# Moving four half turns of expert work out of the query stage, and the prompt's pick into a block of its own

## What is computed

```python
p = rmsnorm(x, ln1) @ w_in                       # qA kA vA | qB kB vB | f | gA gB
yA = band_attention(...); yB = fox_attention(...)
m = sigmoid(gA) * (yA @ w_br_a) + sigmoid(gB) * (yB @ w_br_b)
h = x + m @ w_out
q = rmsnorm(h, ln2) @ w_pq                       # query stage: 8 heads, two halves each
s = q . sub_keys                                 # 2 x 128 scores per head
hs, hi = top_k(s, 16)                            # then the 16 best of the 256 sums
idx, gate = 16 experts per head, softmax of the best sums
a = peer_u[idx] . xn                             # 128 experts per token
h = h + sum(gelu(a) * gate * peer_v[idx])
```

## Time and profile before

| what | value |
| --- | --- |
| median of 3 runs | 2779.17 us |
| the profiled execution | 2783.22 us, its span 2781.3 us |
| TensorE matmul busy | 2244.8 us (81%) |
| VectorE busy | 1832.2 us (66%) |
| GpSimd busy | 1235.1 us (44%) |
| ScalarE busy | 566.9 us (20%) |
| DMA over the span | 1047.28 MB, mean 377 GB/s |
| TensorE clock granted, mean | 0.896 |

### The profile page before, as it was taken

The page is one execution under the profiler, slowest core; times in us unless marked ns, Lnnn a source line. Parts: engine busy times, 40 slices in busy tenths (PEclk is TensorE's granted clock), DMA queues, the critical chain, the costliest instruction groups (busy, mean ns, idle before and its releaser), DMA issues.

```text
span 2781.3 us, 22182 instructions
## 1 busy us (share of the span) xinstructions
PE 2244.8 (81%) x7260; PEld 1189.3 (43%) x7260; DVE 1832.2 (66%) x2636; ACT 566.9 (20%) x1303; POOL 1235.1 (44%) x858
## 2 busy tenths in 40 slices
PE   7999999999999898888799976662340049999996
PEld 3544444444544443333344466662330035444443
DVE  1323001677687866666476899989999997666666
ACT  1222000112222211001001122223996052000000
POOL 2000000034354445444253376666888866444454
PEclk9999999999999999999899988886555578999998
DMA  9887899989899999999999999999999988999998
GB/s 360 320 314 283 275 308 310 330 332 391 339 409 402 399 367 413 410 400 413 378 387 356 412 398 421 421 421 387 406 421 421 422 330 323 408 404 409 409 405 347
DMA packets 271477, 1047.28 MB, mean 377 GB/s; under 512 B 19857, under 2 KB 19857, under 8 KB 203281
## 3 DMA queue, kind: packets, MB, share of 16 engines
q0 software_dynamic: 113792, 697.85, 62.0%
q1 hardware_dynamic: 154880, 343.97, 34.1%
q10 hardware_dynamic: 2704, 4.21, 0.4%
HBM read 1036.50 MB, written 9.45 MB: 376 GB/s over the span
## 4 chain that ended last, share of the span: by engine, by line
PE 37%; DMA 33%; DVE 12%; POOL 10%; issue 6%; ACT 1%; POOLq 0%; SPq 0%; DVEq 0%; ACTq 0%
PE ps L621 33%; DMA yTr<-in_peer_v,fold 13%; POOL bigr L592 7%; DMA bigs<-in_peer_u,fold 7%; DMA bigr<-in_w_in 4%; DMA bigr<-in_w_br_b 4%; DVE hr L1748 3%; DMA bigr<-in_w_out 2%; DMA bigs<-in_peer_v,idxnow 2%; DVE bigs L1717 2%; POOL spare L592 1%; PE ps L937 1%; DMA bigs<-in_peer_u,idxnow 1%; DVE bigr L1717 1%; DVE bigs L1646 1%
## 5 line engine op out<-in xcount | busy, mean ns | idle before, releaser
L621 PE MATMUL ps<-bigr 128*128 128x512 f32 x1920 | 856.0, 604 | 51.2 <-DMA bigr<-in_w_out 20.9
L621 PEld LDWEIGHTS ps<-bigr 128*128 128x128 f32 x1920 | 366.3, 194 | 500.1 <-issue 456.3
L541 POOL DMA_INDIRECT bigs<-in_peer_u,idxnow x128 | 220.2, 1721 | 559.7 <-DVE bigs L1656 543.1
L621 PE MATMUL ps<-bigr,bigs 128*128 128x512 f32 x896 | 404.5, 605 | 25.6 <-DMA bigr<-in_w_in 22.0
L1748 DVE SCALAR_TENSOR_TENSOR hr<-yTr,fold,hr 128x1024 f32<-128x1024 f32 x205 | 263.1, 1284 | 127.2 <-DMA yTr<-in_peer_v,fold 126.0
L1646 DVE SCALAR_TENSOR_TENSOR bigs<-bigs,acts 128x2048 f32<-128x2048 f32 x128 | 300.8, 2350 | 63.8 <-DMA bigs<-in_peer_v,idxnow 63.7
L1656 DVE SCALAR_TENSOR_TENSOR bigs<-bigs 128x2048 f32<-128x2048 f32 x128 | 292.9, 2289 | 72.4 <-DMA bigs<-in_peer_u,idxnow 71.3
L602 POOL DMA_INDIRECT yTr<-in_peer_v,fold x205 | 217.2, 1060 | 200.8 <-DVE hr L1748 191.4
L1717 DVE SCALAR_TENSOR_TENSOR bigr<-bigr 128x2048 f32<-128x2048 f32 x122 | 278.8, 2291 | 17.5 <-DMA bigr<-in_peer_u,fold 16.3
L621 PEld LDWEIGHTS ps<-bigr,bigs 128*128 128x128 f32 x896 | 169.5, 194 | 227.9 <-issue 220.2
L592 POOL DMA_INDIRECT bigr<-in_peer_u,fold x122 | 244.7, 2006 | 43.2 <-issue 37.0
(11 more groups left out here) (276 smaller groups left out, 2382.6 us busy)
## 6 DMA issues: line engine op xcount, KB each, us to landing
bigr<-in_w_in SPq DMA_DIRECT2D x160, 1024.0 KB, 10.1
spare<-in_peer_v SPq DMA_DIRECT2D x96, 512.0 KB, 6.7
bigr<-in_w_out SPq DMA_DIRECT2D x32, 1024.0 KB, 7.7
bigr<-in_w_pq SPq DMA_DIRECT2D x32, 1024.0 KB, 7.3
bigr<-in_w_br_a SPq DMA_DIRECT2D x16, 1024.0 KB, 12.4
bigr<-in_w_br_b SPq DMA_DIRECT2D x16, 1024.0 KB, 10.5
bigr<-in_peer_v SPq DMA_DIRECT2D x32, 512.0 KB, 6.7
bigr<-in_ckT_a POOLq DMA_DIRECT2D x2, 2048.0 KB, 10.6
```

The costliest lines, as they stand in the source:

```text
L541: pool.indirect_dma_start(row, None, table[:, :], bass.IndirectOffsetOnAxis(ap=col, axis=0)).then_inc(loaded, 16)
L621: last = mm(ps[:, bank + t, :], src[:, k0 + k, t * P:(t + 1) * P], wring[:, s, k, :], start=(k0 + k == 0), stop=(k0 + k == kt - 1))
```

## The change

The tables change so that four half turns move out of the query stage: `QUERY_HALVES` (2, 2, 0, 0) is gone; head group 1 gets one more, behind its query norm; pass 0 gets two more, ahead of its first product; output chunk 2 gets one more. In `front` on VectorE, right behind the normalised tokens (L1509), `last_rows` now does the streams' last four additions with nothing between, and then 27 steps of tile 0's pick (three quarters) run in one block. So 10 steps of tile 0 are left for the dots (one of them is `finish`), not 17. The steps on the list are taken off at places 2, 5 and 7 of every 8 as before up to dot place 116, and from there at one place of every 6.

```diff
-HALVES = ((2, 1, 2, 1, 1), (1, 1, 2, 1, 1), (1, 1, 2, 1, 1), (1, 2, 2, 1, 0))
+HALVES = ((2, 1, 2, 1, 1), (2, 1, 2, 1, 1), (1, 1, 2, 1, 1), (1, 2, 2, 1, 0))
 PICK_HALVES = (0, 1, 1, 0)
-PASS_HALVES = ((1, 1, 2), (4, 1, 2), (4, 1, 2), (4, 1, 2))
-OUT_HALVES = (2, 2, 2, 2)
-QUERY_HALVES = (2, 2, 0, 0)
+PASS_HALVES = ((3, 1, 2), (4, 1, 2), (4, 1, 2), (4, 1, 2))
+OUT_HALVES = (2, 2, 3, 2)
...
                     place_query(i)
-                    experts(QUERY_HALVES[i])
                     read_keys(i)
...
                     dve.scalar_tensor_tensor(F.xn2[:, t, :], F.h[:, t, :], rstd[:, 1, t0 + t:t0 + t + 1], ln2b,
                                              ALU.mult, ALU.mult).then_inc(F.xn2_ready, 1)
-                for i in range(NCH):
-                    experts(QUERY_HALVES[i], between if i else None)
+                last_rows()
+                for i in range(1, NCH):
+                    pick_steps(STEPS)
...
-                    if between:
-                        between(3)
-
-            def last_rows(E, tau, h, between):
-                expert_acts(E, tau)
+
+            def last_rows():
+
+                expert_acts(ES, TURNS)
                 for s in range(TURN):
-                    add_row(E, tau, s, h)
-                    between(2)
+                    add_row(ES, TURNS, s, S.h[:, 0, :])
...
-                if at % 8 in (2, 5, 7) and len(stages) > 1:
+                if (at % 8 in (2, 5, 7) if at < DIAGS * EACH else at % 6 == 5) and len(stages) > 1:
                     stages.pop(0)()
```

More of the change, by code:

```diff
@@ L1357, in forget_gate, with front @@
                                          ALU.subtract).then_inc(F.lf_ready, 1)
-            def front(F, experts, between=None):
+            def front(F, experts, last_rows, pick_steps):
                 n, t0 = F.n, F.tiles[0]
@@ L1646, in add_row, with expert_turn @@
                 dve.scalar_tensor_tensor(h, E.vrow[s], acts[:, s:s + 1], h, ALU.mult, ALU.add).then_inc(E.v_free, 1)
-            def expert_turn(E, tau, xn, h, first=False, slots=range(TURN), between=None):
+            def expert_turn(E, tau, xn, h, first=False, slots=range(TURN)):
                 NU = len(E.urow)
@@ L1659, in expert_turn, with stream_turns @@
                         add_row(E, tau, s, h)
-                    if between:
-                        between(3)
-            def last_rows(E, tau, h, between):
-                expert_acts(E, tau)
+            def last_rows():
+                expert_acts(ES, TURNS)
                 for s in range(TURN):
-                    add_row(E, tau, s, h)
-                    between(2)
+                    add_row(ES, TURNS, s, S.h[:, 0, :])
             prepare(S)
-            front(S, lambda *_: None)
+            front(S, lambda *_: None, lambda: None, lambda *_: None)
             dve.wait_ge(made, CONSTS)
             streams_place = Place()
-            def stream_turns(halves, between=None):
+            def stream_turns(halves):
                 for tau, half in streams_place.next(halves):
                     expert_turn(ES, tau, S.xn2[:, 0, :], S.h[:, 0, :], first=streams_place.first(tau),
-                                slots=range(half * TURN // 2, (half + 1) * TURN // 2), between=between)
+                                slots=range(half * TURN // 2, (half + 1) * TURN // 2))
             NU, NV = len(ES.urow), len(ES.vrow)
@@ L1696, in pick_steps @@
                     stages.pop(0)()
-            front(R, stream_turns, pick_steps)
+            front(R, stream_turns, last_rows, pick_steps)
             assert TURNS == streams_place.turns
-            last_rows(ES, TURNS, S.h[:, 0, :], pick_steps)
             finish_first = stages.pop()
```

## The result

The changed kernel takes 2795.9 us (median of 4 runs, 2794.16 to 2801.60), the kernel before 2779.07 us beside it: the ratio is 1.0068 (95% interval 1.0052 to 1.0083). It is slower by 0.68%: 16.8 us by the medians, where +9.6 was forecast. The profiled execution of the changed kernel is its slowest run, 2801.6 us with a span of 2799.7. That span is 18.4 us longer than the one profiled before; 14.7 us of it are there by the last u gather, and no run here tells what the other 3.7, behind the dots, come from.

The account below looks back on a forecast made before the run. No single engine was taken to bound the kernel: bytes bound the passes, TensorE's matmuls the query stage. Terms 0.6 + 13 + 1 + 1.5 - 6.5 = +9.6 us gave 2788.8 us on the median; range 2771 to 2800.

Parts of the forecast that it names:

- Steps 1 and 3: One more half turn each in head group 1 (+0.6 us) and output chunk 2 (+1 us), mostly fitting DMA's room.
- Step 2: Two more half turns ahead of pass 0's first products: 5.5 MB find no DMA room, +13 us.
- Step 4: Query stage without 16.8 MB: TensorE's waits for w_pq go, giving back 3.0 us at its end, 1.7 at quarter 2's keys.
- Step 5: Pick alone with 27 steps ahead of the prompt's dots, not 20: first dot later, +1.5 us.
- Step 6: Seam between the prompt's two tiles: fewer pick steps ahead of dot 128 win back 6.5 of 8.1 us.
- A: Faster: pass 0's weights don't suffer, added gathers only fill VectorE's wait; 2770 to 2776 us, chance 0.20 for below 2773.6.
- B: No change, 2779 us: the bytes' delay is eaten by DMA room at 1380 to 1400 us; chance 0.22.
- C: Slower still, near 2799 us: odd half-turn counts add three gelu waits of VectorE, 9.9 us; chance 0.08.

Follow-up runs that it names:

- the two small moves and the late rule: Kernel before, one query-stage half turn each to head group 1 and output chunk 2, pick steps at one dot place in six from 116: 2769.92 us.
- The kernel with plain loads: Kernel before plus four plain 2 MB loads issued by ScalarE around pass 0's first three chunks, no VectorE or GpSimd work added: 2795.98 us.
- pass 0 alone: Kernel before with only two half turns moved from the query stage to ahead of pass 0's first products: 2787.78 us.
- The kernel with 26 us of multiplications: Kernel before plus 46 VectorE multiplications of a scratch tile ahead of pass 0's half turns, no bytes or half turns moved: 2790.97 us.
- the late rule alone: Kernel before with only pick steps taken off at one dot place in six from place 116, all half turns staying: 2772.32 us.
- the block alone: Kernel before, half turns staying in the query stage, last additions and 27 pick steps in one block behind them, sparser steps from place 116: 2794.95 us.

## Why the prediction came out as it did

The direction and the mechanism of the largest term were right; the size was 7 us short. By the medians the change is: the two small moves and the late rule -7.8, the block +8.2, pass 0 +16.4, together +16.8. The prediction's "terms' own bounds make 2783 to 2800" is not their sum: added up, its bounds reach from -9 to +29.5 us, from 2770 to 2809 on the median. Of its signs, the stretch from 1000 to 1040 us is full (412 GB/s), output chunk 0 is 14.9 us late for 10 to 14, and the query stage is down to 342 GB/s.

**Steps 1 and 3** (+0.6, +1): right within what can be told: alone, with what they take out of the query stage, they are worth -1.8, and that includes the 5 us that a lighter stage gives back, so the moves themselves cost some 3.

**Step 2** (+13): right in kind, some 3 us short. The kernel with plain loads says that it is bytes without room, with the reservation made there: 8.39 MB cost 16.4 us. With pass 0 alone it was 9.3 and the 5 us that its lighter query stage gave back, 14. The sum counted only the 5.5 MB / 409 GB/s. What it left out is seen in TensorE: between 1000 us and output chunk 0, 14.9 us longer after, its idle time grew by 2.2 us only (60.6 to 62.9), and its matmuls got longer.

```profile
L620 PE MATMUL ps<-bigr 128*128 128x512 f32 x465 | 217.2, 627 | 31.0 <-DMA bigr<-in_w_in 23.7 <-DMA bigr<-in_w_out 7.3
L620 PE MATMUL ps<-bigr,yTr 128*128 128x512 f32 x256 | 120.6, 631 | 31.8 <-DMA bigr<-in_w_br_a 19.0 <-DMA bigr<-in_w_br_b 9.5 <-ACT bigr L1110 3.3
```

In the same stretch of before (to 1388.12 us) these groups have:

```profile
L621 PE MATMUL ps<-bigr 128*128 128x512 f32 x455 | 209.1, 619 | 33.9 <-DMA bigr<-in_w_in 19.8 <-DMA bigr<-in_w_out 13.4 <-ACT bigr L1102 0.8
L621 PE MATMUL ps<-bigr,yTr 128*128 128x512 f32 x256 | 115.9, 610 | 26.7 <-DMA bigr<-in_w_br_a 17.7 <-DMA bigr<-in_w_br_b 5.7 <-ACT bigr L1111 3.3
```

Neighbouring matmuls overlap, so their mean durations (616 and 629 ns over both groups) don't add up to time; busy time over count does, 325.0 / 711 = 457 ns before and 337.8 / 721 = 469 ns after, 11.4 ns x 721 = 8.2 us. The granted clock of the passes fell from 0.95 to 0.92. Ten matmuls fewer are recorded of before. If they are missing records, each counts as idle, 4.6 us in all, and then an estimate is 8 us of longer matmuls and 7 us of wait; no run here shows that they are.

Also short was the reason beside it, "that alone is hidden" of VectorE's own lateness. The kernel with 26 us of multiplications loses 13.3 us. The lateness is harmless to TensorE, as the step said, but VectorE is what frees the gathers' buffers, so its time too turns into room that DMA doesn't use. In the change this loss isn't seen, since the work in question is the gathers' own and DMA is full (412 GB/s).

The rule of the Trainium skill (DMA: Bandwidth & Descriptors, Queues, rings and completion order) that was weighed there isn't contradicted: from 1000 to 1040 us the weights' queue moved 5.61 MB before and 4.18 MB after, while the gathers' rose from 7.81 to 12.28 MB. But with the 26 us of multiplications the weights moved 4.83 MB there although DMA was down at 214 GB/s, so only the fall from there to 4.18 speaks for the gathers. And four plain loads in a third queue left the weights 4.97 MB and cost as much. So the rule may tell who is late in the first 40 us, and not what the whole costs.

**Step 4** (gives back 1.7): not in the change. The scores of quarter 2 were 16.9 us late where the stage began 16.3 late. The waits for `w_pq` didn't vanish, they moved to the stage's start (0.92 and 1.17 us). That a lighter stage can give back more, if the pick stays woven in, is shown by the kernel with pass 0 alone (6.0 us from scores to first dot for 10.8): "VectorE wasn't what the stage waited for" was true of TensorE and not of the first dot. In the earlier trace rows quarter 2's first step begins at 1603.38, 5 us behind its scores at 1598.50, because quarter 1's last steps and the additions, themselves behind the half turns, stand in front. I had both rows and read past them.

**Step 5** (+1.5): the arithmetic held to the microsecond, scores at 1615.50 plus a block of 13.3 us is the first dot at 1628.83, and against the stage's start it is +3.8 with the 1.7 that weren't given back (the prediction's sign was 1 to 2). That it came so near is partly luck: two things that it left out, 5 us from a lighter stage and 8 for the block, nearly cancel. The step compared the block with an old arrangement that was 5 us late for another reason, and so hid its price. Against a kernel as light the block costs 8 us: it puts nine steps of quarter 2 ahead of the first dot, where two are enough (1594.77 to 1600.11 us in the kernel of the small moves and the late rule), while eight full buffers wait. In the changed kernel DMA runs at 92 GB/s meanwhile.

**Step 6** (-6.5): right in place and nearly in size. From the first dot to the last u gather 5.4 us were won, and alone the rule brings 5 to 6. GpSimd's wait shrank to 3.89 us, not to 2; with the late rule alone it stayed at 6.95 for the same gain, so this wait is no measure of it.

**The rivals.** A (the weights don't suffer) falls with output chunk 0 at 1403.05. B's sign came true to the letter, 414 GB/s for 208 at 1380 to 1400 us, but not its outcome: as much opened elsewhere, 354 at 1400 to 1420 and, in the 20 us slices of the passes, 282 at 1140 to 1160. The sign was a poor one, and so was the row: the late rule alone and the block alone run the same program up to there and moved 386 and 374 GB/s in that stretch, so the room of 4.0 MB belonged to the one execution that was profiled and not to the kernel. C (gelu waits) falls: VectorE's only such wait in the passes is 0.37 us, where before had 3.30.

## What to carry to other kernels

Where a stretch is full of DMA, price a move by bytes against the room between its new place and the next stretch that isn't full, and look for that room in more than one execution; an engine's wait in front of the new place is no room, and work on the engine that frees the transfers' buffers uses up room even if it moves no byte. When the pick for a ring of buffers is put in a block, count how many of its steps the first consumer needs and let the ring run behind those; everything more stands between full buffers and their release. And compare a step with the same arrangement without it, not with the old kernel: a part that is slow there for another reason hides its price.

## What the hardware showed unexpectedly

A wait of TensorE for weights is dearer than its length: 16 matmuls of 128x512 took 7.13 us behind a short wait and 9.17 to 9.28 us behind waits of 9.33 and 4.85 us. Of the 20 us slices between 1000 and 1480 us of the kernel after, 16 have TensorE standing and starting again, and 11 of these show a granted clock of 0.83 to 0.93 (one 0.74, four 1.00); the eight in which it is busy throughout all show 1.00, which is 2.4 GHz. The kernel before has one exception, 0.91 in a stretch busy throughout (1380 to 1400 us). Two slices of the kernel after:

```profile
1080.00:1100.00 20.00, 16.01 (x30) 6.39 (x28) 14.74 (x10) 1.49 (x2) 11.77 (x8) 0.83 1.02 413
1140.00:1160.00 20.00, 20.00 (x48) 8.92 (x47) 13.43 (x14) 0.00 (x0) 7.27 (x5) 1.00 0.76 282
```

So in these rows late weights cost some 2 us on top of a longer wait.
